# Gate and up projections of a SwiGLU network on one core: eight of eleven chunks computed with the weights stationary, their results kept in columns

## The chip, the cores and the metric

The kernel runs on one core of one Trainium2 chip. The metric is the time of one execution in device microseconds; of three runs of the kernel before the median is 706.38 us (705.44 to 707.03). A profile is one execution, recorded instruction by instruction.

## The reference

Two transformer layers over 256 rows of 1024 channels, all in float32. Each layer is an attention block, a layer norm, a SwiGLU network and a second layer norm. The change touches only the network:

```
def swiglu(h, wg, wu, wd):                      # h 256x1024, wg and wu 1024x2816, wd 2816x1024
    return (jax.nn.silu(h @ wg) * (h @ wu)) @ wd
```

## The kernel before

**Precision.** Float32 accuracy is had from three products of a rounded type: every operand is split into hi (rounded to fp32r) and lo (the rest), and `product` (L969 to L973) issues hi x hi, hi x lo and lo x hi into the same place of PSUM. Each `nc.tensor.matmul(dst, stationary, moving)` loads a 128x128 stationary block into the array (LDWEIGHTS, the profile's engine PEld) and streams the columns of the moving operand through it (MATMUL, engine PE). The profile's names put the moving operand first: `ps<-w_hi,a_lo` is a product that moves w_hi past stationary a_lo.

**The stream of weights.** All weights come from one array of units of 128x2048 values (1 MB). SyncE loads unit u into `raw[u % 3]`; ScalarE rounds it to `w_hi` (`round_unit`, L389); VectorE forms `w_lo` (`rest_of_unit`, L650); TensorE uses it and raises `w_used`. Three slots are in use in turn. Each engine has its own program; their order is only set by the semaphores in it.

**The network.** `ffn` stands once per engine (ScalarE L556, VectorE L910, TensorE L1210) and runs twice, once per layer. The hidden width 2816 is cut into 11 chunks (NFC) of 256. A chunk c takes three units: two of gate and up weights (one for each half of the 1024 channels; in each unit four k tiles of 128 channels, each with 256 gate and 256 up columns), and one of down weights. The activations, already turned, lie as `a_hi`/`a_lo[channel, half, k tile, row]`, half being one of two groups of 128 rows.

For one chunk TensorE issues, before the change:

- `chunk` (L994): for each unit, each half and each k tile, a product with the activations stationary and 512 columns of weights moving: 2 x 2 x 4 x 3 = 48 matmuls of 512 columns. Results have rows on partitions: PSUM bank 0 is half 0, bank 1 is half 1, each with 256 gate and 256 up values.
- `down` (L1218) of the chunk before, with the hidden values stationary: 2 x 2 x 2 x 3 = 24 matmuls of 512 columns into banks 4 to 7, which sum over all chunks.
- `turn_hidden` (L1226): four transposes (128x128, `nc.tensor.transpose` at L1230) that bring the hidden rows of this chunk into columns, as the down product needs them, in PSUM bank 2 (`hT_ps`).

ScalarE takes the silu of the gate half (`silu_of`, L558), VectorE multiplies it by the up half into `h_rows` (`hidden`, L911), TensorE turns, ScalarE rounds the turned values from PSUM into `h_hi` (`hidden_hi`, L562), VectorE forms `h_lo` (`hidden_lo`, L916). Between these each of them rounds the next units, in a fixed order: unit j=2, silu or hidden, unit j=3, hi or lo, unit j=4. Chunks 2 to 9 are one hardware loop on TensorE (`step`, L1233, under `pe.Fori`, L1256), chunks 1 to 9 one on ScalarE (L577) and VectorE (L931). Chunks 0, 1 and 10 are written out.

Of the kernel before, what the change touches and what calls it, by code (L numbers as in the profile page):

```python
# [21 lines left out]
S = 256  # L22
# [4 lines left out]
HALF = 2  # L27
# [31 lines left out]
def build(nc, x_rows, x_cols, stream, w_gates, w1, w2, cpos, positions, norms, out):  # L59
# [8 lines left out]
    with ExitStack() as ctx:  # L68
# [184 lines left out]

        set_ps = ps[:, 4:6, :].rearrange("p b (t r) -> p (b t) r", r=S)
        hT_ps = ps[:, 2, :].rearrange("p (h t r) -> p h t r", h=HALF, t=2)

        def out_ps(t):

# [124 lines left out]
        def _(act):  # L383
            units = [0]

            def copy(dst, src, scale=1.0):
                return nc.scalar.activation(dst, src, ACT.Copy, scale=scale)  # L387
# [168 lines left out]
            def ffn(u0, c0):  # L556

                def silu_of(c, whole):  # L558
                    act.wait_ge(w_used, whole)
                    nc.scalar.activation(silu[:, :, :], ps[:, 0:2, 0:FC], ACT.Silu).then_inc(silu_ready, 1)  # L560

                def hidden_hi(c, hi=h_hi):  # L562
                    act.wait_ge(hT_done, c0 + c + 1)
                    copy(hi[:, :, :, :], hT_ps).then_inc(h_hi_ready, 1)

                def round_in(c, j):

                    round_unit((u0 + j) % SLOTS, ((u0 + j) // SLOTS + 1) * 16 + c * 16, 3 * c + (u0 + j - 2))

                act.wait_ge(first_sums, u0 // U_FF1 + 1)  # L570
                nc.scalar.activation(silu[:, 0, :], ps[:, 0, 0:FC], ACT.Silu).then_inc(first_silu, 1)
                act.wait_ge(w_used, u0 + 2)
                nc.scalar.activation(silu[:, 1, :], ps[:, 1, 0:FC], ACT.Silu).then_inc(silu_ready, 1)
                round_to(u0 + 4)
                hidden_hi(0)
                round_to(u0 + 5)
                with act.Fori(1, NFC - 1) as c:  # L577
                    round_in(c, 2)
                    silu_of(c, 3 * c + (u0 + 1))
                    round_in(c, 3)  # L580
                    hidden_hi(c)
                    round_in(c, 4)
                units[0] = u0 + 3 * (NFC - 1) + 2
                c = NFC - 1
                round_to(u0 + 3 * c + 3)
                silu_of(c, u0 + 3 * c + 1)
                hidden_hi(c, last_hi)
                round_to(min(UNITS, u0 + 3 * c + 5))

            def nsa_values():  # L590
# [41 lines left out]
        def _(dve):  # L632
# [21 lines left out]
            def rest_to(end):  # L654
                for u in range(units[0], end):
                    rest_of_unit(u % SLOTS, u + 1)
                units[0] = max(units[0], end)
# [252 lines left out]
            def ffn(u0, c0):  # L910
                def hidden(c):  # L911
                    dve.wait_ge(silu_ready, c0 + c + 1)
                    nc.vector.tensor_tensor(h_rows[:, :, :], silu[:, :, :], ps[:, 0:2, FC:2 * FC],  # L913
                                            ALU.mult).then_inc(h_ready, 1)

                def hidden_lo(c, hi=h_hi, lo=h_lo):  # L916
                    dve.wait_ge(h_hi_ready, c0 + c + 1)
                    minus(lo[:, :, :, :], hT_ps, hi[:, :, :, :].bitcast(f32)).then_inc(h_lo_ready, 1)

                def rest_in(c, j):  # L920

                    rest_of_unit((u0 + j) % SLOTS, 3 * c + (u0 + j + 1))

                dve.wait_ge(first_silu, u0 // U_FF1 + 1)
                nc.vector.tensor_tensor(h_rows[:, 0, :], silu[:, 0, :], ps[:, 0, FC:2 * FC], ALU.mult).then_inc(first_h, 1)
                dve.wait_ge(silu_ready, c0 + 1)
                nc.vector.tensor_tensor(h_rows[:, 1, :], silu[:, 1, :], ps[:, 1, FC:2 * FC], ALU.mult).then_inc(h_ready, 1)
                rest_to(u0 + 4)
                hidden_lo(0)
                rest_to(u0 + 5)  # L930
                with dve.Fori(1, NFC - 1) as c:  # L931
                    rest_in(c, 2)
                    hidden(c)
                    rest_in(c, 3)
                    hidden_lo(c)
                    rest_in(c, 4)
                units[0] = u0 + 3 * (NFC - 1) + 2
                c = NFC - 1
                rest_to(u0 + 3 * c + 3)
                hidden(c)  # L940
                hidden_lo(c, last_hi, last_lo)
                rest_to(min(UNITS, u0 + 3 * c + 4))

# [24 lines left out]
        def _(pe):  # L968
# [25 lines left out]
            def chunk(u, banks, count=None):  # L994


                for unit in range(2):
                    one_unit(u, unit, banks, count=count)
# [211 lines left out]
            def ffn(u0, c0, ready, l):  # L1210
                def down_part(s, half, k, hi, lo, start, stop, c):


                    at = slice(1024 * k + 512 * c, 1024 * k + 512 * (c + 1))
                    return product(ps[:, 4 + 2 * half + c, :], hi[:, half, k, :], lo[:, half, k, :],
                                   w_hi[:, s, at], w_lo[:, s, at], start=start, stop=stop)

                def down(s, start):  # L1218

                    for half in range(HALF):  # L1220
                        for k in range(2):
                            for c in range(2):
                                last = down_part(s, half, k, h_hi, h_lo, start and k == 0, False, c)
                    last.then_inc(w_used, 1)

                def turn_hidden(c):  # L1226
                    pe.wait_ge(h_ready, c0 + c + 1)
                    for half in range(HALF):
                        for t in range(2):
                            last = nc.tensor.transpose(hT_ps[:, half, t, :], h_rows[:, half, P * t:P * (t + 1)], ident[:, :])  # L1230
                    last.then_inc(hT_done, 1)

                def step(c):  # L1233

                    chunk(u0 + 2, (0, 1), count=3 * c + (u0 - 1))
                    pe.wait_ge(h_lo_ready, c0 + c)
                    pe.wait_ge(lo_ready, 3 * c + (u0 + 2))
                    down((u0 + 1) % SLOTS, False)
                    turn_hidden(c)

                first_chunk(u0, ready, l)

                pe.wait_ge(lo_ready, u0 + 3)
                pe.wait_ge(first_h, u0 // U_FF1 + 1)
                rows_by_weights(u0 + 2, 0, 0, 0)
                turn_hidden(0)
                rows_by_weights(u0 + 2, 0, 1, 1).then_inc(w_used, 1)
                pe.wait_ge(lo_ready, u0 + 4)
                for half in range(HALF):
                    last = rows_by_weights(u0 + 3, 1, half, half)  # L1250
                last.then_inc(w_used, 1)
                pe.wait_ge(h_lo_ready, c0 + 1)
                pe.wait_ge(lo_ready, u0 + 5)
                down((u0 + 4) % SLOTS, True)
                turn_hidden(1)
                with pe.Fori(2, NFC - 1) as c:  # L1256
                    step(c)


                c = NFC - 1  # L1260
                s_before, s_last = (u0 + 3 * c + 1) % SLOTS, (u0 + 3 * c + 2) % SLOTS
                chunk(u0 + 3 * c - 1, (0, 1))
                pe.wait_ge(h_lo_ready, c0 + c)
                pe.wait_ge(lo_ready, u0 + 3 * c + 2)
                for cols in range(2):
                    down_part(s_before, 0, 0, h_hi, h_lo, False, False, cols)
                turn_hidden(c)
                for cols in range(2):
                    down_part(s_before, 0, 1, h_hi, h_lo, False, False, cols)
                pe.wait_ge(h_lo_ready, c0 + NFC)  # L1270
                pe.wait_ge(lo_ready, u0 + 3 * NFC)
                for cols in range(2):
                    for k in range(2):
                        last = down_part(s_last, 0, k, last_hi, last_lo, False, k == 1, cols)
                    last.then_inc(sums_done, 1)
                for k in range(2):
                    for cols in range(2):
                        last = down_part(s_before, 1, k, h_hi, h_lo, False, False, cols)
                last.then_inc(w_used, 1)
                for cols in range(2):  # L1280
                    for k in range(2):
                        last = down_part(s_last, 1, k, last_hi, last_lo, False, k == 1, cols)
                    last.then_inc(sums_done if cols == 0 else w_used, 1)
                if l + 1 < 3:
                    turn_x(l + 1, 0)
# [121 lines left out]
```

## Time and profile before

| | before |
|---|---|
| median of three runs | 706.38 us (705.44 to 707.03) |
| span of the profiled execution | 704.3 us; its own time is not given apart from the span |
| TensorE (PE) busy | 675.0 us, 96% |
| weight loads (PEld) busy | 545.7 us, 77% |
| VectorE (DVE) busy | 405.2 us, 58% |
| ScalarE (ACT) busy | 307.6 us, 44% |
| mean DMA rate | 160 GB/s |

The span runs from the first to the last instruction. Busy is the union of the recorded instructions of an engine. A record of a matmul begins when the instruction is taken up and its end is modelled, so consecutive matmuls overlap in the records: what one costs is the distance between the starts of two neighbours, here called the pitch, and not its length. PE and PEld work side by side.

### The profile page before, as it was taken

The page shows a single profiled execution, that of the slowest core. Times are in us where ns is not written, and L with a number is a line of the kernel's source. Part 1 is how long each engine was busy: PE and PEld are TensorE (multiplying, and loading weights), DVE is VectorE, ACT ScalarE, POOL GpSimd, SP SyncE. Part 2 cuts the span into 40 slices and gives each one's busy share as a digit, 9 for nine tenths or more (in the row PEclk, how much of TensorE's full clock was granted, in tenths as well). Part 3 has the DMA queues.
Part 4 walks back from the last instruction along what each step waited for, and adds up shares of the span by engine and source line. Part 5 has one row for each costly group of instructions (what it writes and reads, how often), then busy time and mean ns, then how long its engine had stood idle before and what let it go on. Part 6 is the DMA issues. An engine that isn't in the chain of part 4 may idle for free.

```text
span 704.3 us, 8489 instructions
## 1 busy us (share of the span) xinstructions
PE 675.0 (96%) x3180; PEld 545.7 (77%) x3180; DVE 405.2 (58%) x529; ACT 307.6 (44%) x435; POOL 30.5 (4%) x66
## 2 busy tenths in 40 slices
PE   5899999999999999999998999999989999999995
PEld 4686886778778888888876788778768888888884
DVE  4554377774864444455448656585855455444446
ACT  4633537663353444433343454674344433334430
POOL 4001000000120000000002000000110000000001
PEclk9999989999999999999999999999999999999998
DMA  8954122003355555555443645313246555555501
GB/s 298 422 198 179 61 83 97 1 2 120 119 191 228 185 185 199 198 186 179 179 179 121 239 180 180 137 43 106 97 165 244 200 197 186 179 182 185 201 27 60
DMA packets 18282, 112.97 MB, mean 160 GB/s; under 512 B 2768, under 2 KB 3024, under 8 KB 5584
## 3 DMA queue, kind: packets, MB, share of 16 engines
q1 hardware_dynamic: 16384, 103.18, 40.2%
q10 hardware_dynamic: 720, 5.24, 1.9%
q0 software_dynamic: 1152, 4.19, 1.7%
q8 instruction: 17, 0.28, 0.2%
q14 instruction: 9, 0.07, 0.0%
HBM read 111.56 MB, written 1.05 MB: 160 GB/s over the span
## 4 chain that ended last, share of the span: by engine, by line
PE 84%; DVE 9%; POOL 2%; DMA 2%; ACT 1%; SPq 1%; issue 1%; POOLq 0%; DVEq 0%
PE ps L971 22%; PE ps L972 22%; PE ps L973 22%; PE ps L1128 4%; PE ps L1163 3%; DVE w_lo L648 2%; PE ps L1076 2%; DMA raw<-stream 2%; PE ps L1230 1%; PE ps L1143 1%; DVE bn L864 1%; PE ps L1165 1%; DVE x L859 1%; DVE x L882 1%; POOL rstd L365 1%
## 5 line engine op out<-in xcount | busy, mean ns | idle before, releaser
L648 DVE TENSOR_TENSOR w_lo<-raw,w_hi 128x2048 fp32r<-128x2048 f32 (+1 forms) x98 | 220.1, 2248 | 134.2 <-ACT w_hi L387 133.9
L971 PE MATMUL ps<-w_hi,a_hi 128*128 128x512 f32 x592 | 238.6, 403 | 15.2 <-DVE w_lo L648 11.2
L972 PE MATMUL ps<-w_lo,a_hi 128*128 128x512 f32 x592 | 233.4, 394 | 0.0
L387 ACT ACTIVATE w_hi<-raw 128x2048 fp32r<-128x2048 f32 (+1 forms) x98 | 184.1, 1878 | 112.5 <-PE ps L973 104.7
L973 PE MATMUL ps<-w_hi,a_lo 128*128 128x512 f32 x592 | 233.2, 394 | 0.0
L971 PEld LDWEIGHTS ps<-w_hi,a_hi 128*128 128x128 f32 x592 | 112.8, 191 | 41.9 <-DVE w_lo L648 11.7
L973 PEld LDWEIGHTS ps<-w_hi,a_lo 128*128 128x128 f32 x592 | 112.8, 191 | 24.5
L972 PEld LDWEIGHTS ps<-w_lo,a_hi 128*128 128x128 f32 x592 | 113.1, 191 | 22.1
L971 PE MATMUL ps<-w_hi,h_hi 128*128 128x512 f32 x160 | 62.4, 390 | 0.0
L973 PE MATMUL ps<-w_hi,h_lo 128*128 128x512 f32 x160 | 62.3, 390 | 0.0
L972 PE MATMUL ps<-w_lo,h_hi 128*128 128x512 f32 x160 | 62.2, 389 | 0.0
L560 ACT ACTIVATE arena<-ps 128x512 f32<-128x512 f32 x20 | 12.0, 598 | 70.3 <-PE ps L973 70.3
L513 ACT ACTIVATE arena<-ps,neg_max 128x128 f32<-128x128 f32 (+1 forms) x96 | 39.0, 427 | 3.4 <-DVE neg_max L798 3.3
L387 ACT ACTIVATE h_hi<-ps 128x512 fp32r<-128x512 f32 x20 | 12.0, 599 | 64.5 <-PE ps L1230 64.5
L1128 PE MATMUL ps<-kz,qT 128*128 128x256 f32 (+1 forms) x96 | 37.6, 488 | 0.0
L973 PEld LDWEIGHTS ps<-w_hi,h_lo 128*128 128x128 f32 x160 | 30.0, 188 | 6.2
L972 PEld LDWEIGHTS ps<-w_lo,h_hi 128*128 128x128 f32 x160 | 30.0, 188 | 6.2
L971 PEld LDWEIGHTS ps<-w_hi,h_hi 128*128 128x128 f32 x160 | 30.0, 188 | 6.2
L913 DVE TENSOR_TENSOR arena<-arena,ps 128x512 f32<-128x512 f32 x20 | 13.8, 688 | 36.4 <-ACT arena L560 36.4
L387 ACT ACTIVATE arena<-ps 128x512 f32<-128x512 f32 (+1 forms) x30 | 18.2, 612 | 37.6 <-PE ps L1147 30.2
L648 DVE TENSOR_TENSOR h_lo<-ps,h_hi 128x512 fp32r<-128x512 f32 x20 | 13.8, 691 | 32.1 <-ACT h_hi L387 32.1
L363 POOL TENSOR_SCALAR var_eps<-mean_var 128x1 f32<-128x1 f32 x8 | 6.0, 748 | 603.6 <-DVE mean_var L869 603.6
(146 smaller groups left out, 570.2 us busy)
## 6 DMA issues: line engine op xcount, KB each, us to landing
raw<-stream SPq DMA_DIRECT2D x94, 1024.0 KB, 4.8
gain<-norms POOLq DMA_DIRECT2D x8, 512.0 KB, 5.0
arena<-w ACTq DMA_DIRECT2D x4, 1024.0 KB, 8.4
raw<-stream SPq DMA_DIRECT2D x4, 512.0 KB, 8.0
twice<-x_cols SPq DMA_DIRECT2D x4, 256.0 KB, 7.1
x<-x_rows ACTq DMA_DIRECT2D x1, 1024.0 KB, 4.8
out<-x SPq DMA_DIRECT2D x4, 256.0 KB, 2.0
wg_raw<-w_gates SPq DMA_DIRECT2D x1, 192.0 KB, 9.6
```

The source lines that it names most:

```text
L365: nc.gpsimd.tensor_tensor(rstd[:, l, half:half + 1], var_eps[:, l, half:half + 1], minus_half[:, :], ALU.pow).then_inc(rstd_ready, 1)
L387: return nc.scalar.activation(dst, src, ACT.Copy, scale=scale)
L513: last = nc.scalar.activation(probs[:, b, at:at + keys], ps[:, 2 - 2 * half + b, h * keys:(h + 1) * keys], ACT.Exp, bias=neg_max[:, j0 + i ...
L560: nc.scalar.activation(silu[:, :, :], ps[:, 0:2, 0:FC], ACT.Silu).then_inc(silu_ready, 1)
L648: return nc.vector.tensor_tensor(dst, a, b, ALU.subtract)
L913: nc.vector.tensor_tensor(h_rows[:, :, :], silu[:, :, :], ps[:, 0:2, FC:2 * FC], ALU.mult).then_inc(h_ready, 1)
L971: nc.tensor.matmul(dst, hi, m_hi, start=start, stop=False)
L972: nc.tensor.matmul(dst, hi, m_lo, start=False, stop=False)
L973: return nc.tensor.matmul(dst, lo, m_hi, start=False, stop=stop)
L1076: last = nc.tensor.matmul(ps[0:KV * NCMP, 6, HID * kv:HID * (kv + 1)], blocks[:, kv, j, :, :].rearrange("p g n -> p (g n)"), w1_sb[:, kv, ...
L1128: nc.tensor.matmul(dst, qT[:, q, P * half:P * (half + 1)], kz[:, k, :, 0:keys], start=True, stop=False)
L1163: nc.tensor.matmul(dst, values[:, 0, c], probsT[:, b, S * h:S * (h + 1)], start=j0 > 0 and h == 0, stop=False)
```

## The change

Chunks 2 to 9 of both layers (16 chunks) compute gate and up the other way round. `columns_by_weights` takes a 128x128 block of the weights as the stationary operand and moves the 256 activation columns (both halves, 2 x 128) past it: per k tile four blocks (two of gate, two of up) and three products each, 2 x 4 x 4 x 3 = 96 matmuls of 256 columns for a chunk. Results have the hidden unit on the partition and the row in the column: bank 0 holds gate, bank 1 up. So silu and the product with up give `h_columns`, a view of the same memory as `h_rows`, which is already in the layout that `down` needs, and these chunks have no `turn_hidden`. `h_hi` and `h_lo` are made from it in SBUF, not from PSUM. `columns_hi` on ScalarE waits for the down product of the chunk before (`w_used`), `hidden_columns` on VectorE waits for `columns_lo` of the chunk before (`h_lo_ready`), and TensorE waits for `h_ready` of the chunk before at the start of a step. Chunks 0, 1 and 10 stay as they were; chunk 1 is now written out on ScalarE and VectorE too. `hT_done` now counts three turns for each network.

```diff
--- before.py
+++ after.py
@@ -253,6 +253,9 @@
 
         set_ps = ps[:, 4:6, :].rearrange("p b (t r) -> p (b t) r", r=S)
         hT_ps = ps[:, 2, :].rearrange("p (h t r) -> p h t r", h=HALF, t=2)
+        h_columns = h_rows.rearrange("p t (h r) -> p t h r", h=HALF)
+
+        TURNS = 3
 
         def out_ps(t):
 
@@ -559,9 +562,19 @@
                     act.wait_ge(w_used, whole)
                     nc.scalar.activation(silu[:, :, :], ps[:, 0:2, 0:FC], ACT.Silu).then_inc(silu_ready, 1)
 
-                def hidden_hi(c, hi=h_hi):
-                    act.wait_ge(hT_done, c0 + c + 1)
+                def silu_columns(c):
+                    act.wait_ge(w_used, 3 * c + (u0 + 1))
+                    nc.scalar.activation(silu[:, :, :], ps[:, 0, :].rearrange("p (t r) -> p t r", t=2),
+                                         ACT.Silu).then_inc(silu_ready, 1)
+
+                def hidden_hi(turned_hidden, hi=h_hi):
+                    act.wait_ge(hT_done, turned_hidden)
                     copy(hi[:, :, :, :], hT_ps).then_inc(h_hi_ready, 1)
+
+                def columns_hi(c):
+                    act.wait_ge(h_ready, c0 + c + 1)
+                    act.wait_ge(w_used, 3 * c + (u0 + 2))
+                    copy(h_hi[:, :, :, :].rearrange("p h t r -> p t h r"), h_columns).then_inc(h_hi_ready, 1)
 
                 def round_in(c, j):
 
@@ -572,19 +585,24 @@
                 act.wait_ge(w_used, u0 + 2)
                 nc.scalar.activation(silu[:, 1, :], ps[:, 1, 0:FC], ACT.Silu).then_inc(silu_ready, 1)
                 round_to(u0 + 4)
-                hidden_hi(0)
+                hidden_hi(TURNS * (u0 // U_FF1) + 1)
                 round_to(u0 + 5)
-                with act.Fori(1, NFC - 1) as c:
+                round_in(1, 2)
+                silu_of(1, u0 + 4)
+                round_in(1, 3)
+                hidden_hi(TURNS * (u0 // U_FF1) + 2)
+                round_in(1, 4)
+                with act.Fori(2, NFC - 1) as c:
                     round_in(c, 2)
-                    silu_of(c, 3 * c + (u0 + 1))
+                    silu_columns(c)
                     round_in(c, 3)
-                    hidden_hi(c)
+                    columns_hi(c)
                     round_in(c, 4)
                 units[0] = u0 + 3 * (NFC - 1) + 2
                 c = NFC - 1
                 round_to(u0 + 3 * c + 3)
                 silu_of(c, u0 + 3 * c + 1)
-                hidden_hi(c, last_hi)
+                hidden_hi(TURNS * (u0 // U_FF1) + 3, last_hi)
                 round_to(min(UNITS, u0 + 3 * c + 5))
 
             def nsa_values():
@@ -913,6 +931,18 @@
                     nc.vector.tensor_tensor(h_rows[:, :, :], silu[:, :, :], ps[:, 0:2, FC:2 * FC],
                                             ALU.mult).then_inc(h_ready, 1)
 
+                def hidden_columns(c):
+                    dve.wait_ge(silu_ready, c0 + c + 1)
+                    dve.wait_ge(h_lo_ready, c0 + c)
+                    nc.vector.tensor_tensor(h_columns, silu[:, :, :].rearrange("p t (h r) -> p t h r", h=HALF),
+                                            ps[:, 1, :].rearrange("p (t h r) -> p t h r", t=2, h=HALF),
+                                            ALU.mult).then_inc(h_ready, 1)
+
+                def columns_lo(c):
+                    dve.wait_ge(h_hi_ready, c0 + c + 1)
+                    minus(h_lo[:, :, :, :].rearrange("p h t r -> p t h r"), h_columns,
+                          h_hi[:, :, :, :].rearrange("p h t r -> p t h r").bitcast(f32)).then_inc(h_lo_ready, 1)
+
                 def hidden_lo(c, hi=h_hi, lo=h_lo):
                     dve.wait_ge(h_hi_ready, c0 + c + 1)
                     minus(lo[:, :, :, :], hT_ps, hi[:, :, :, :].bitcast(f32)).then_inc(h_lo_ready, 1)
@@ -928,15 +958,21 @@
                 rest_to(u0 + 4)
                 hidden_lo(0)
                 rest_to(u0 + 5)
-                with dve.Fori(1, NFC - 1) as c:
+                rest_in(1, 2)
+                hidden(1)
+                rest_in(1, 3)
+                hidden_lo(1)
+                rest_in(1, 4)
+                with dve.Fori(2, NFC - 1) as c:
                     rest_in(c, 2)
-                    hidden(c)
+                    hidden_columns(c)
                     rest_in(c, 3)
-                    hidden_lo(c)
+                    columns_lo(c)
                     rest_in(c, 4)
                 units[0] = u0 + 3 * (NFC - 1) + 2
                 c = NFC - 1
                 rest_to(u0 + 3 * c + 3)
+                dve.wait_ge(h_lo_ready, c0 + c)
                 hidden(c)
                 hidden_lo(c, last_hi, last_lo)
                 rest_to(min(UNITS, u0 + 3 * c + 4))
@@ -1230,13 +1266,27 @@
                             last = nc.tensor.transpose(hT_ps[:, half, t, :], h_rows[:, half, P * t:P * (t + 1)], ident[:, :])
                     last.then_inc(hT_done, 1)
 
+                def columns_by_weights(u, unit):
+
+                    s = u % SLOTS
+                    for k in range(4):
+                        kt = 4 * unit + k
+                        for j in range(4):
+                            at = slice(512 * k + P * j, 512 * k + P * (j + 1))
+                            last = product(ps[:, j // 2, S * (j % 2):S * (j % 2 + 1)], w_hi[:, s, at], w_lo[:, s, at],
+                                           a_hi[:, :, kt, :], a_lo[:, :, kt, :], start=kt == 0 and j % 2 == 0,
+                                           stop=kt == KT - 1 and j % 2 == 1)
+                    last.then_inc(w_used, 1)
+
                 def step(c):
 
-                    chunk(u0 + 2, (0, 1), count=3 * c + (u0 - 1))
+                    pe.wait_ge(h_ready, c0 + c)
+                    for unit in range(2):
+                        pe.wait_ge(lo_ready, 3 * c + (u0 + unit))
+                        columns_by_weights(u0 + 2 + unit, unit)
                     pe.wait_ge(h_lo_ready, c0 + c)
                     pe.wait_ge(lo_ready, 3 * c + (u0 + 2))
                     down((u0 + 1) % SLOTS, False)
-                    turn_hidden(c)
 
                 first_chunk(u0, ready, l)
 
@@ -1259,6 +1309,7 @@
 
                 c = NFC - 1
                 s_before, s_last = (u0 + 3 * c + 1) % SLOTS, (u0 + 3 * c + 2) % SLOTS
+                pe.wait_ge(h_ready, c0 + c)
                 chunk(u0 + 3 * c - 1, (0, 1))
                 pe.wait_ge(h_lo_ready, c0 + c)
                 pe.wait_ge(lo_ready, u0 + 3 * c + 2)
```

## Rows read from the trace of the kernel before

**Rows 1.** The page: span, busy time of TensorE, and the chain that ended last.

```profile
span 704.3 us, 8489 instructions
...
PE 675.0 (96%) x3180; PEld 545.7 (77%) x3180; DVE 405.2 (58%) x529; ACT 307.6 (44%) x435; POOL 30.5 (4%) x66
...
PE 84%; DVE 9%; POOL 2%; DMA 2%; ACT 1%; SPq 1%; issue 1%; POOLq 0%; DVEq 0%
```

**Rows 2.** Windows, chunks 2 to 9 of each layer; columns as in the first line.

```profile
core 0: us, PE busy (x) PEld busy (x) DVE busy (x) ACT busy (x) POOL busy (x), PEclk, DMA share, GB/s
217.90:352.40 134.50, 134.50 (x611) 111.33 (x610) 66.07 (x40) 53.80 (x40) 0.00 (x0) 1.00 0.53 187
538.30:672.80 134.50, 134.50 (x612) 111.33 (x610) 66.07 (x40) 53.80 (x40) 0.00 (x0) 1.00 0.52 187
```

**Rows 3.** Timeline of PE, one chunk of the loop: start us, length us.

```profile
251.38 0.60 PE L1230 MATMUL ps<-ident,arena 128*128 128x128 f32 x4
251.73 0.48 PE L971 MATMUL ps<-w_hi,a_hi 128*128 128x512 f32 x1
252.05 0.40 PE L972 MATMUL ps<-w_lo,a_hi 128*128 128x512 f32 x1
...
252.52 0.40 PE L971 MATMUL ps<-w_hi,a_hi 128*128 128x512 f32 x1
...
254.36 0.39 PE L973 MATMUL ps<-w_hi,a_lo 128*128 128x512 f32 x1
...
267.96 0.39 PE L973 MATMUL ps<-w_hi,h_lo 128*128 128x512 f32 x1
268.19 0.60 PE L1230 MATMUL ps<-ident,arena 128*128 128x128 f32 x4
```

**Rows 4.** Timeline of ScalarE and VectorE in two chunks of the loop.

```profile
246.13 0.60 ACT L560 ACTIVATE arena<-ps 128x512 f32<-128x512 f32 x1 [3.52 <-PE ps L973]
246.76 0.69 DVE L913 TENSOR_TENSOR arena<-arena,ps 128x512 f32<-128x512 f32 x1 [1.83 <-ACT arena L560]
252.01 0.60 ACT L387 ACTIVATE h_hi<-ps 128x512 fp32r<-128x512 f32 x1 [3.48 <-PE ps L1230]
252.65 0.69 DVE L648 TENSOR_TENSOR h_lo<-ps,h_hi 128x512 fp32r<-128x512 f32 x1 [1.78 <-ACT h_hi L387]
254.45 2.29 DVE L648 TENSOR_TENSOR w_lo<-raw,w_hi 128x2048 fp32r<-128x2048 f32 x1 [1.11 <-ACT w_hi L387]
```

**Rows 5.** Timeline, products with 48 moving columns (the gates of the attention).

```profile
32.81 0.19 PEld L973 LDWEIGHTS ps<-wg_hi,a_lo 128*128 128x128 f32 x1
32.84 0.27 PE L973 MATMUL ps<-wg_hi,a_lo 128*128 128x48 f32 x1
32.92 0.19 PEld L971 LDWEIGHTS ps<-wg_hi,a_hi 128*128 128x128 f32 x1
...
33.71 0.19 PEld L972 LDWEIGHTS ps<-wg_lo,a_hi 128*128 128x128 f32 x1
```

**Rows 6.** Timeline of PE in the attention: plain f32 and bf16 products.

```profile
113.01 0.38 PE L1165 MATMUL ps<-arena 128*128 128x128 f32 x2
113.23 0.60 PE L1128 MATMUL ps<-kz,qT 128*128 128x256 f32 x2
113.66 0.27 PE L1130 MATMUL ps<-causal,ident_b 128*128 128x256 bf16 x1
113.77 0.59 PE L1128 MATMUL ps<-kz,qT 128*128 128x512 f32 x1
```

**Rows 7.** The loads of those products: the groups of PEld by shape, x is their number.

```profile
L1165 PEld LDWEIGHTS ps<-arena 128*128 128x128 f32 x96 | 18.2, 190 | 2.5
```

**Rows 8.** A window in which the granted clock is 0.50; columns as in rows 2.

```profile
387.96:391.37 3.41, 3.41 (x9) 2.64 (x10) 2.69 (x2) 0.00 (x0) 0.00 (x0) 0.50 0.72 285
```

**Rows 9.** Timeline of PE in that window.

```profile
388.37 0.63 PE L972 MATMUL ps<-w_lo,a_hi 128*128 128x512 f32 x1
...
390.93 0.60 PE L972 MATMUL ps<-w_lo,a_hi 128*128 128x512 f32 x1
```

## The prediction

> **What bounds the kernel now.** I read the page first: span 704.3 us, TensorE busy for 675.0 us of it and 84% of the chain that ended last [rows 1]. The reader is to see that no other engine is near: VectorE has 58%, ScalarE 44%. But a mean over stages doesn't price a change to one of them, so next the windows: in the loop over chunks 2 to 9, both layers, PE is busy for 134.50 of 134.50 us, VectorE for 66.07, ScalarE for 53.80, the DMA share is 0.53 and the granted clock 1.00, the upper level, 2.4 GHz [rows 2]. TensorE never waits there. So the change is worth what it does to TensorE's own instruction stream in 2 x 134.5 us, and nothing else, as long as no wait opens.
>
> Busy time says nothing of what a matmul costs, so the third view is the timeline: start to start. From the first turn of one chunk (251.38) to that of the next (268.19) are 16.81 us [rows 3]. In between stand 4 turns and 72 matmuls of 512 columns. From the 12th of these (254.36) to the 72nd (267.96) are 60 steps in 13.60 us: a pitch of 226.7 ns [rows 3]. 512 columns at 2.4 GHz are 213.3 ns, so each matmul pays 13.4 ns beyond its columns. On these 13.4 ns the forecast hangs.
>
> **What goes.** 72 x 226.7 ns = 16.32 us; the chunk takes 16.81; so the four turns and the switch around them cost 0.49 us [rows 3]: 0.35 from the first turn to the next matmul (251.38 to 251.73), 0.09 because that matmul takes 0.32 instead of 0.23, and 0.05 in the ten or so that follow. 16 chunks: 7.8 us. All of it lies on the path, since PE never rests [rows 2]. The turns wait for nothing now, so no stall goes with them. If the slow matmuls after a switch remain (the shape still switches twice in a chunk, 512 to 256 and back), 0.05 us stay per switch: 0.8 to 1.6 us less gain. I take zero and keep 1.6 for the range.
>
> **What comes.** 48 matmuls of 512 columns become 96 of 256, three products for each of 32 (block, k tile) pairs. The columns are the same, 24,576 per chunk; the number of matmuls and of weight loads doubles. In 16 chunks 768 matmuls at 226.7 ns = 174.1 us become 1536 at a pitch p. With the turns gone,
>
> change of the time = 1536 x p - 174.1 - 7.8 us.
>
> No row shows an fp32r matmul of 256 columns, so p is bounded from the nearest rows.
>
> - *The load.* Each matmul needs a load of 128 columns of 32 bits. With only 48 columns moving, eight loads take 32.81 to 33.71: 112 ns each [rows 5]. That is the load's own pace, and p can't be under it. It does hide behind a matmul: in the attention two f32 matmuls of 128 columns with such loads (190 ns long in the record) take 113.01 to 113.23, 110 ns each [rows 6, 7], where a pass over 128 f32 columns costs half of the 256-column pass, itself 0.43 / 2 = 215 ns [rows 6]. Load and stream, both about 107 ns, run side by side at full overlap. It is just this balance that the changed chunks will have.
> - *The stream.* 256 columns at 2.4 GHz are 106.7 ns. A bf16 matmul of 256 columns takes 113.66 to 113.77, 110 ns, with the load of a f32 matmul behind it [rows 6]. So 256 columns in full-rate mode aren't slow as such.
> - *The 13.4 ns.* They are seen with fp32r at the full clock only. At a granted clock of 0.50 (1.2 GHz) the same matmul of 512 columns takes 388.37 to 390.93 for six, 426.7 ns [rows 8, 9], which is 512 / 1.2 with nothing over. The f32 pass of 256 columns at full clock, two cycles for a column, takes 215 ns against 213 [rows 6]. So the extra is no work of the array: it shows only when the array draws 32-bit columns at 2.4 GHz, and hides as soon as it draws half as fast. Either what feeds the columns needs a restart for each instruction that a slower array doesn't notice (a fixed 13.4 ns for each matmul, p = 120.1), or it feeds 6% too slowly (in proportion, p = 113.3).
>
> I take the fixed cost. A feed that is too slow by just 6% for a clock that differs twofold from the next one would be a coincidence; an instruction's start that has slack at half rate and none at full rate is what the three rows ask for. Both ends stay: 112 ns (load bound) and, above, 128 (below).
>
> Sum: 1536 x 120.1 ns = 184.5 us; 184.5 - 174.1 - 7.8 = +2.6 us. The changed chunk takes 96 x 0.120 + 24 x 0.2267 = 16.97 us against 16.81. The doubled number of starts costs 0.64 us in a chunk, more than the 0.49 that the turns gave.
>
> The Trainium skill (TensorE: Matmul & The Clock Gate, Back-to-back issue gap) gives N / 2.4 + 2.5 ns for a warm matmul, a fixed part too, but a small one. The bf16 row agrees with it within the timeline's 10 ns [rows 6]; the fp32r stream doesn't: 226.7 against 215.8 ns [rows 3]. By that rule p would be 109 ns, under the load's 112, so the load would decide: this is the second rival.
>
> **Edits that I price at nothing.** Silu, the product, hi and lo keep their number and size (128x512: 0.60, 0.69, 0.60, 0.69 us [rows 4]); two of them now read SBUF instead of PSUM, whose price the trace doesn't show for ScalarE. They have room. The new wait of `columns_hi` for the down product ends at about the time of the old one: `h_hi` starts at 252.01 behind four turns that start at 251.38, as the down product ends [rows 3, 4]. `h_lo` is there by 253.34, and the down product that needs it starts 48 matmuls after 251.73, at 262.7: 9 us of cover [rows 3, 4]. Behind the waiting `columns_hi` on ScalarE stands the rounding of unit j=4, and VectorE's rest of it, done at 256.74 [rows 4] and needed at 262.7 also: 6 us of cover. TensorE's new wait for `h_ready`: `hidden` ends at 247.45 [rows 4], the step begins at 251.7, 4 us of cover; behind it would stand the whole step. `hidden_columns` waits for `columns_lo` of the chunk before, an instruction ahead of it in VectorE's own order. Units are used in the same order at the same times within 2%, so SyncE's loads, 0.53 of the DMA time [rows 2], don't move. If one such cover failed, each us would be paid 16 times; I see none within 4 us of failing.
>
> **Rivals.**
>
> 1. *In proportion (faster).* p = 113.3: the streams stay at 174.1 and the 7.8 us of turns are pure gain: -7.8, 698.6 us. For it: 226.7 is 17/16 of 213.3, and a rate is the simplest reading of one size. Against: the two half-rate rows above.
> 2. *Load bound (faster).* The extra belongs to matmuls longer than their load, or is small; p = 112: 172.0 - 174.1 - 7.8 = -9.9, 696.5 us. For it: the f32 and bf16 rows at 110 [rows 6]. Against: nothing there draws fp32r.
> 3. *Never settled (slower).* The matmuls behind a switch run late: the 12th starts at 254.36, where ten pitches from the second, at 252.05, would give 254.32, and the two steps from 252.05 to 252.52 take 235 ns each, 21.7 over the columns [rows 3]. The stream takes some ten matmuls to reach its even pace, at which each load begins with the matmul before it and has 120 ns of slack. With 256 columns moving there is no slack: load 112, stream 107. If the pace after a switch is the pace throughout, p = 106.7 + 21.7 = 128: 196.6 - 174.1 - 7.8 = +14.7, 721 us. It decides for slower from p = 118.4 on, where the turns are used up. TensorE's instruction supply would work in the same direction: pairs of load and matmul stand at 110 ns only in short runs here [rows 5, 6], and the change asks for 96 at 120.
> 4. *Loads in the open.* p = 107 + 112 = 219: 336.4 - 174.1 - 7.8 = +154, 861 us. The rows speak against it: 226.7 is far less than 213 + 112 [rows 3, 5], and two of 110 ns hold a load and a pass each [rows 6]. The Trainium skill (TensorE: Matmul & The Clock Gate, The mechanism) says that a weight load overlaps a running matmul only where it goes to other rows of the array, and here all rows are used both times; by that rule this rival would be the forecast. The trace contradicts it.
>
> That the change doesn't do what it says could only mean that turns stay; the steps have none left, so I give that no chance.
>
> **How the numbers follow.** The sum is a difference, made in the profiled execution (704.3 us of span); the median of the runs is 706.38, 2.1 us higher, and the difference is put on it. Fixed cost, with p from 118.5 to 124: 0.40, forecast 706.38 + 2.6 = 709.0. In proportion: 0.23. Load bound: 0.12. Never settled, p over 124: 0.19. Loads in the open: 0.02. Something that cancels (p from 117.5 to 118.5, or a mix): 0.04. What a measurement can tell from no change is about 0.2%, 1.4 us, so same means p between 117.5 and 119.3; part of the fixed case lies there. Faster: 0.23 + 0.12 + 0.02 = 0.37. Same: 0.08. Slower: 0.55. The range: down to the load bound's 696.5, up to the never-settled 721, leaving half of each tail out. The forecast's own range, p from 118.5 to 124, is 706.5 to 715.
>
> **What would show it.** In the changed timeline the start-to-start of 256-column matmuls in the middle of a step: 120 ns right, 113 or 112 the first or second rival, 128 the third. The period of a chunk, between matmuls of the same place: 16.97 us against 16.81. PE busy throughout the loop's windows: the covers held. No L1230 between chunk 1 and chunk 10. If PE shows idle time before the first matmul of a step, a wait that I priced at nothing is the cause and the forecast is wrong in that step; if the pitch of the 512-column matmuls of `down` moves from 226.7, my fixed price is no property of a matmul, and the reasoning falls even if the sum should hold.

## The result, and the profile after

The changed kernel takes 707.91 us (median of 18 runs, 705.28 to 709.92) against 705.46 us of the kernel before (18 runs beside it): 2.5 us more by the medians. The ratio on record, which need not be the quotient of the two medians, is 1.0044, with a 95% interval of 1.0026 to 1.0061: 3.1 us slower, 1.8 to 4.3. The forecast was 2.6 us slower.

The page of the changed kernel, against [rows 1]:

```profile
span 705.2 us, 9901 instructions
...
PE 675.5 (96%) x3884; PEld 577.7 (82%) x3884; DVE 405.2 (57%) x529; ACT 307.9 (44%) x435; POOL 30.4 (4%) x66
...
PE 84%; DVE 9%; POOL 2%; DMA 2%; ACT 1%; SPq 1%; issue 1%; POOLq 0%; DVEq 0%
```

There are 704 more matmuls and as many more loads (768 more, and 64 turns fewer); VectorE and ScalarE are as they were. The page can't show more: its span is only 0.9 us longer. The windows by stage do. Chunks 2 to 9 of both layers, the stage between the two, the start, and one chunk (columns as in [rows 2]):

```profile
219.36:355.28 135.92, 135.92 (x963) 128.25 (x962) 66.09 (x40) 53.98 (x40) 0.00 (x0) 1.00 0.51 185
537.92:673.83 135.91, 135.91 (x963) 128.25 (x962) 66.08 (x40) 54.01 (x40) 0.00 (x0) 1.00 0.51 185
355.28:523.85 168.57, 162.13 (x773) 129.17 (x772) 111.25 (x163) 80.64 (x129) 9.04 (x12) 1.00 0.41 150
0.00:75.73 75.73, 64.16 (x308) 50.22 (x308) 35.03 (x47) 32.02 (x32) 10.80 (x43) 0.98 0.66 255
236.42:253.40 16.98, 16.98 (x121) 16.02 (x120) 8.26 (x5) 6.75 (x5) 0.00 (x0) 1.00 0.50 185
```

The same stages of the kernel before, as far as the groups ahead don't hold them:

```profile
352.55:524.41 171.86, 165.44 (x775) 131.58 (x774) 111.27 (x163) 80.68 (x129) 9.05 (x12) 0.98 0.41 147
0.00:74.46 74.46, 63.23 (x308) 49.53 (x309) 35.06 (x47) 32.07 (x32) 10.82 (x43) 1.00 0.69 259
218.13:352.55 134.42, 134.42 (x611) 111.25 (x610) 66.07 (x40) 53.80 (x40) 0.00 (x0) 1.00 0.53 187
538.50:672.93 134.43, 134.43 (x611) 111.26 (x610) 66.07 (x40) 53.80 (x40) 0.00 (x0) 1.00 0.52 187
```

The reader is to see that PE is busy for all of 135.92 us, so no wait opened, and that the changed stage grew from 134.42 to 135.92 us, in the second layer from 134.43 to 135.91 (+2.98 in all), which lies inside the measured 1.8 to 4.3. The stages that didn't change differ too. The one between the layers has -3.29 us, and PE's busy time alone has -3.31 (162.13 against 165.44); the start has +1.27, of which PE's busy time has 0.93. The same matmuls took another time because the granted clock was another (1.00 against 0.98 between the layers, 0.98 against 1.00 at the start): the spells at 1.2 GHz fall in other places from one execution to the next. Comparing the spans of two executions would have hidden two thirds of the effect.

The timeline of PE in one changed chunk, against [rows 3]:

```profile
236.42 0.28 PE L1007 MATMUL ps<-a_hi,w_hi 128*128 128x256 f32 x1
236.53 0.28 PE L1008 MATMUL ps<-a_lo,w_hi 128*128 128x256 f32 x1
...
247.81 0.28 PE L1009 MATMUL ps<-a_hi,w_lo 128*128 128x256 f32 x1
247.93 0.40 PE L1007 MATMUL ps<-w_hi,h_hi 128*128 128x512 f32 x1
...
250.45 0.39 PE L1009 MATMUL ps<-w_hi,h_lo 128*128 128x512 f32 x1
...
253.17 0.39 PE L1009 MATMUL ps<-w_hi,h_lo 128*128 128x512 f32 x1
253.40 0.28 PE L1007 MATMUL ps<-a_hi,w_hi 128*128 128x256 f32 x1
```

From the 2nd to the 96th, 94 steps in 11.28 us: 120.0 ns. The down product keeps its 24 matmuls, in 5.47 us, and from 250.45 to 253.17 they have the pitch of before: 12 steps in 2.72 us, 226.7 ns. No turn stands at 253.40. The period, from the first matmul of a chunk to the first of the next, is 16.98 us, 0.17 more than before.

ScalarE and VectorE in the same chunk, against [rows 4]:

```profile
248.13 0.60 ACT L567 ACTIVATE arena<-ps 128x512 f32<-128x512 f32 x1 [3.85 <-PE ps L1009]
248.76 0.69 DVE L937 TENSOR_TENSOR arena<-arena,ps 128x512 f32<-128x512 f32 x1 [2.15 <-ACT arena L567]
253.60 0.63 ACT L390 ACTIVATE h_hi<-arena 128x512 fp32r<-128x512 f32 x1 [3.07 <-PE ps L1009]
254.26 0.69 DVE L666 TENSOR_TENSOR h_lo<-arena,h_hi 128x512 fp32r<-128x512 f32 x1 [1.40 <-ACT h_hi L390]
256.07 2.29 DVE L666 TENSOR_TENSOR w_lo<-raw,w_hi 128x2048 fp32r<-128x2048 f32 x1 [1.11 <-ACT w_hi L390]
```

`h_hi` from SBUF takes 0.63 us instead of 0.60. The product with up (L937) ends at 249.45, 4 us ahead of the step at 253.40; `h_lo` ends at 254.95, 10 us ahead of the down product that uses it (264.91), and the rest of unit j=4 at 258.36, 6.5 us ahead of the same. The covers held.

### The profile page after: what moved, and what is told of

Read it like the earlier page. It is cut to its first block, busy times and chain, and to the rows that moved or that the text cites. A ratio compares the mean times of both kernels' runs of the same rounds, so it can differ in the third digit from the quotient of the medians.

```text
span 705.2 us, 9901 instructions
## 1 busy us (share of the span) xinstructions
PE 675.5 (96%) x3884; PEld 577.7 (82%) x3884; DVE 405.2 (57%) x529; ACT 307.9 (44%) x435; POOL 30.4 (4%) x66
## 4 chain that ended last, share of the span: by engine, by line
PE 84%; DVE 9%; POOL 2%; DMA 2%; ACT 1%; SPq 1%; issue 1%; POOLq 0%; DVEq 0%
PE ps L1007 23%; PE ps L1009 22%; PE ps L1008 22%; PE ps L1164 4%; PE ps L1199 3%; DVE w_lo L666 2%; PE ps L1112 2%; DMA raw<-stream 2%; PE ps L1179 1%; DVE bn L882 1%; PE ps L1201 1%; DVE x L877 1%; DVE x L900 1%; POOL rstd L368 1%; DVE a_lo L666 1%
## 5 line engine op out<-in xcount | busy, mean ns | idle before, releaser
L1007 PE MATMUL ps<-w_hi,a_hi 128*128 128x512 f32 x336 | 136.3, 406 | 15.6 <-DVE w_lo L666 11.6
L1007 PE MATMUL ps<-a_hi,w_hi 128*128 128x256 f32 x512 | 145.0, 283 | 0.0
L1009 PE MATMUL ps<-a_hi,w_lo 128*128 128x256 f32 x512 | 144.9, 283 | 0.0
L1008 PE MATMUL ps<-a_lo,w_hi 128*128 128x256 f32 x512 | 144.9, 283 | 0.0
L1009 PE MATMUL ps<-w_hi,a_lo 128*128 128x512 f32 x336 | 133.0, 396 | 0.0
L1008 PE MATMUL ps<-w_lo,a_hi 128*128 128x512 f32 x336 | 132.8, 395 | 0.0
L1008 PEld LDWEIGHTS ps<-a_lo,w_hi 128*128 128x128 f32 x512 | 98.2, 192 | 0.5
L1007 PEld LDWEIGHTS ps<-a_hi,w_hi 128*128 128x128 f32 x512 | 98.2, 192 | 0.5
L1009 PEld LDWEIGHTS ps<-a_hi,w_lo 128*128 128x128 f32 x512 | 98.2, 192 | 0.0
L1009 PEld LDWEIGHTS ps<-w_hi,a_lo 128*128 128x128 f32 x336 | 64.1, 191 | 14.0
```

What stands on the lines that cost most here:

```text
L1007: nc.tensor.matmul(dst, hi, m_hi, start=start, stop=False)
L1008: nc.tensor.matmul(dst, hi, m_lo, start=False, stop=False)
L1009: return nc.tensor.matmul(dst, lo, m_hi, start=False, stop=stop)
```

## The experiments

Each was made from one of the two kernels; times are compared with the kernel before on the same chip. Where one execution was taken, the verdict rests on the pitch, or on the period of a chunk, and not on the time. From the second chunk of a layer on the period repeats within 0.01 us, with half loads in the kernel before within 0.04. Where a run computes only a part of the chunks or takes other operands, only its time is read. In the cuts from the edits, `...` stands for what is left out.

**The turns back in the changed kernel.**

```diff
                     down((u0 + 1) % SLOTS, False)
+                    pe.wait_ge(h_ready, c0 + c + 1)
+                    for half in range(HALF):
+                        for t in range(2):
+                            nc.tensor.transpose(hT_ps[:, half, t, :], h_rows[:, half, P * t:P * (t + 1)], ident[:, :])
```

> The changed kernel with four turns put back at the end of each step of chunks 2 to 9 (their result goes to bank 2 and isn't used). Theory of the forecast, that turns and the switch around them cost 0.49 us and the doubled starts 0.64 us of a chunk: period 16.98 + 0.45 to 0.49 = 17.43 to 17.47 us, time 7.2 to 7.8 us above the changed kernel, 1.5% above the kernel before. Rival, that the turns were nearly free because the switch between shapes costs the same with and without them (the changed kernel still switches twice): period up by 0.35 or less, 5.6 us or less.

Measured 714.74 us, ratio 1.0144 (1.0118 to 1.0171). The windows of two chunks:

```profile
219.24:236.66 17.42, 17.42 (x128) 16.41 (x126) 8.25 (x5) 6.87 (x6) 0.00 (x0) 1.00 0.52 182
236.66:254.07 17.41, 17.41 (x128) 16.40 (x126) 8.26 (x5) 6.75 (x6) 0.00 (x0) 1.00 0.51 181
```

The second, 17.41, is 0.43 over 16.98: just under what was expected (0.45 to 0.49) and over the rival's 0.35. The timeline splits it into 0.35 from the first turn to the next matmul and 0.08 because that matmul takes 0.20 instead of 0.12. (The first chunk of a layer stands behind the turns of chunk 1 in the changed kernel too, where it takes 17.06, 219.36 to 236.42; so 17.42 isn't to be compared with 16.98.) By the two ratios the time is 1.0% or 7 us above the changed kernel. The turns were no free work.

**The turns out of the kernel before.**

```diff
+                def stale_hi(c):
+                    act.wait_ge(w_used, 3 * c + (u0 + 2))
+                    copy(h_hi[:, :, :, :], hT_ps).then_inc(h_hi_ready, 1)
...
-                    hidden_hi(c)
+                    stale_hi(c)
...
                 def step(c):
 
+                    pe.wait_ge(h_ready, c0 + c)
...
-                    turn_hidden(c)
```

> The kernel before with the turns of chunks 2 to 9 left out and nothing else: the down products of these chunks use hidden values of chunk 1 that still stand in bank 2, so that part of the computation is left out. Theory of the forecast: the period falls from 16.81 to 72 x 226.7 ns = 16.32 us, 7.8 us faster than the kernel before, a ratio of 0.989. Rival (the turns hide behind the matmuls, or uncover a wait for the weights): a period of 16.6 to 16.81, 0 to 3 us faster.

Measured 695.56 us, ratio 0.9877 (0.9851 to 0.9904). A window of one chunk:

```profile
249.98:266.30 16.32, 16.32 (x74) 13.51 (x72) 8.26 (x5) 6.72 (x5) 0.00 (x0) 1.00 0.56 193
```

16.32 us, as worked out from the pitch. The ratio gives 8.7 us (6.8 to 10.5), which holds the 7.8 expected. So the turns are worth 0.49 us a chunk, and the 96 short matmuls in place of 48 long ones cost the 0.66 us between 16.32 and 16.98: 0.64 by the two pitches (96 x 120.0 - 48 x 226.7 ns), and 0.02 at the change of shape.

**One run of 256 moving columns in place of two of 128.**

```diff
-                                           a_hi[:, :, kt, :], a_lo[:, :, kt, :], ...
+                                           a_hi[:, 0, min(kt, 6):min(kt, 6) + 2, :], a_lo[:, 0, min(kt, 6):min(kt, 6) + 2, :], ...
```

> The changed kernel with the 256 moving columns taken from two neighbouring k tiles of one half, one run of 256 in place of two runs of 128 (so gate and up of chunks 2 to 9 are products with other activations). Theory (a fixed price for each matmul): a pitch of 120.0 ns as in the changed kernel. Rival (the price is for each run of addresses, or the two runs add to it): the pitch falls, to 113 if half of the 13.3 ns belongs to each run; time 10 us less.

Measured in one execution: 708.09 us; the timeline of PE, 2nd and 96th matmul of a chunk:

```profile
253.20 0.28 PE L1008 MATMUL ps<-a_lo,w_hi 128*128 128x256 f32 x1
...
264.48 0.28 PE L1009 MATMUL ps<-a_hi,w_lo 128*128 128x256 f32 x1
```

11.28 / 94 = 120.0 ns. Whether the 256 columns are one run of addresses or two makes no difference.

**384 moving columns.** The same edit with three k tiles, `ps[:, j // 2, 0:384]` as the target.

> The changed kernel with 384 moving columns in one run in place of 256 (other activations, results over one another). Theory (columns at 2.4 GHz plus 13.3 ns): 173.3 ns, the kernel 82 us longer than the changed one, 789 us. Rival (the stream is 17/16 too slow, which 512 fits as well, and 256 is set by the load): 170.0 ns, 5 us less than that.

Measured 787.87 us in one execution. The 8th and the 96th matmul:

```profile
263.25 0.33 PE L1008 MATMUL ps<-a_lo,w_hi 128*128 128x384 f32 x1
...
278.50 0.33 PE L1009 MATMUL ps<-a_hi,w_lo 128*128 128x384 f32 x1
```

15.25 / 88 = 173.3 ns, that is 384 / 2.4 = 160.0, and 13.3. With 256 (120.0) and 512 (226.7) three sizes lie on one line: the columns at 2.4 GHz, and 13.3 ns for each matmul. The rival's proportion (170.0) is out.

**128 moving columns, twice as many matmuls.** Each product of the changed chunks is issued once for each half.

> The changed kernel with each matmul of 256 columns cut into two of 128 (192 matmuls of 128 columns for a chunk). Theory: the stream would take 53.3 + 13.3 = 66.7 ns, so the load decides, 111 to 112 ns; a chunk takes 192 x 0.112 + 5.44 = 26.9 us, the kernel about 160 us more than the changed one, 867 us. Rival (price of the start adds to the load, the two don't overlap): 112 + 13 = 125 ns, 40 us more than that.

Measured 866.13 us in one execution; a chunk takes 26.94 us:

```profile
271.64:298.58 26.94, 26.94 (x218) 25.95 (x216) 8.26 (x5) 6.75 (x5) 0.00 (x0) 1.00 0.33 117
```

From the 2nd to the 192nd matmul of this chunk (271.70 to 292.91) are 190 steps in 21.21 us, 111.6 ns. 128 columns and the 13.3 ns would be 66.7, so something else sets the pitch: the load's own pace, the 112 of [rows 5]. Nothing is added to it; the rival's 125 is out.

**Half of the load.** Stationary blocks of 64 columns, everything else alike.

```diff
-                            at = slice(512 * k + P * j, 512 * k + P * (j + 1))
-                            last = product(ps[:, j // 2, ...
+                            at = slice(512 * k + P * j, 512 * k + P * j + 64)
+                            last = product(ps[0:64, j // 2, ...
```

> The changed kernel with stationary blocks of 64 columns in place of 128 in the changed chunks (half of gate and up isn't computed), the moving columns and the number of matmuls the same. Theory (the 13.3 ns belong to the moving stream's start): the pitch stays at 120.0 ns although the load is half as long. Rival (with 256 columns the load fills the pitch and sets it, 112 ns and something for the handover, and the agreement with 106.7 + 13.3 is chance): the pitch falls, to 113.3 by the proportion or 109 without any price, 10 to 17 us less.

Measured 695.13 us in one execution. The 2nd and the 96th matmul of a chunk:

```profile
250.35 0.28 PE L1008 MATMUL ps<-a_lo,w_hi 128*64 128x256 f32 x1
...
261.01 0.28 PE L1009 MATMUL ps<-a_hi,w_lo 128*64 128x256 f32 x1
```

10.66 / 94 = 113.4 ns. This speaks against the forecast's reading: the moving stream is the same, and half of the 13.3 ns is gone. The edit halves two things at once, though: what is loaded, and the partitions of PSUM that a matmul writes (64 in place of 128). No run parts them while fp32r moves. The value that the rival named came true, though its reading (a load that sets the pitch) doesn't fit 384 and 512 columns.

**The changed chunks in bf16.** Weights and activations as `.bitcast(bf16)`, every other element.

> The changed kernel with weights and activations of the changed chunks read as bf16 (the upper half of each value, every other element, so the low parts of the products lose their worth). Theory (the price belongs to 32-bit columns at the full clock): 109 to 110 ns, 15 to 17 us less than the changed kernel, about 692 us. Rival (any matmul of 256 full-rate columns beside a load of 128 pays it in a long stream, and the single bf16 matmul in the attention didn't show it): 120 ns, no change.

Measured 701.52 us in one execution, with a mean granted clock of 0.984 against 0.989 in the changed kernel, so the time says little. The 2nd and the 96th matmul of a chunk:

```profile
253.34 0.27 PE L1008 MATMUL ps<-a_lo,w_hi 128*128 128x256 bf16 x1
...
263.99 0.28 PE L1009 MATMUL ps<-a_hi,w_lo 128*128 128x256 bf16 x1
```

10.65 / 94 = 113.3 ns. Neither theory: a long bf16 stream pays 6.7 ns, which the single bf16 matmul of [rows 6], read as one step of 0.11 us, couldn't show. Single steps at a change of type also mislead: the step out of this bf16 stream is 0.03 us (263.99 to 264.02) and the one behind it 0.32. So the price isn't that of 32-bit columns alone. Both operands are read here with a stride of two elements; whether that has a part wasn't tested. With the half loads it made a new theory: the load's bytes set it.

**A quarter of the load.** As above, with 32 columns.

> The changed kernel with stationary blocks of 32 columns in the changed chunks (three quarters of gate and up aren't computed). Theory now (the extra over the columns is the load's: 13.3 ns for 128 columns of 32 bits, 6.7 for 64 columns, 6.7 for 128 columns of 16 bits, so one cycle of 2.4 GHz for each 16 bytes that a partition's load reads): 106.7 + 3.3 = 110.0 ns, a period of about 10.56 + 5.44 + 0.03 = 16.03 us, the kernel 15 us under the changed one. Rival (two levels, a slow and a fast one, and 64 columns already had the fast one): 113.3 ns as with 64 columns, 10 us under.

Measured 707.65 us in one execution, clock 0.984. The 3rd and the 96th matmul of a chunk:

```profile
254.06 0.28 PE L1009 MATMUL ps<-a_hi,w_lo 128*32 128x256 f32 x1
...
265.02 0.28 PE L1009 MATMUL ps<-a_hi,w_lo 128*32 128x256 f32 x1
```

10.96 / 93 = 117.8 ns, 11.2 over the columns: more than with 64 columns. Both theories fall (110.0 and 113.3).

**Half of the load in the kernel before.** Stationary blocks of 64 rows, 512 columns moving: `product(ps[0:64, half, :], a_hi[:, half, kt, 0:64], a_lo[:, half, kt, 0:64], ...)`.

> The kernel before with stationary blocks of 64 rows in gate and up of chunks 2 to 9 (half of the rows aren't computed), 512 weight columns moving as before. Theory (the extra is the load's): 213.3 + 6.7 = 220.0 ns in place of 226.7, a period of 16.49 us, 5 us under the kernel before. Rival (the forecast's reading: 13.4 ns for the start of each 32-bit stream, whatever is loaded): 226.7 ns, a period of 16.81 us, no change.

Measured 707.75 us in one execution. The 3rd and the 48th matmul of a chunk:

```profile
252.15 0.39 PE L973 MATMUL ps<-w_hi,a_lo 128*64 128x512 f32 x1
...
262.49 0.39 PE L973 MATMUL ps<-w_hi,a_lo 128*64 128x512 f32 x1
```

10.34 / 45 = 229.8 ns, more than the 226.7 with the whole load, and the period rose from 16.81 to 16.92 and 16.96 us. Both fall again (220.0 and 226.7). A narrower stationary block, with a shorter load and fewer partitions written, can make the stream slower.

**The wide kernel.** `a_hi` and `a_lo` in one tile, so that a block of w_hi needs one matmul. The order of the blocks changes too: all k tiles of a block come before the next block.

```diff
+                            nc.tensor.matmul(ps[:, j, :], w_hi[:, s, at], a_both[:, :, :, kt, :], start=kt == 0, stop=False)
+                            last = nc.tensor.matmul(ps[:, j, 0:S], w_lo[:, s, at], a_hi[:, :, kt, :], start=False, stop=kt == KT - 1)
```

> The changed kernel with a_hi and a_lo side by side in one tile, so that a stationary block of w_hi takes one matmul of 512 moving columns (a_hi and a_lo) into a bank of its own, and a block of w_lo one of 256 into the first half of that bank; ScalarE copies the second halves out, VectorE adds them. 64 matmuls for a chunk in place of 96, the same columns. Theory (13.3 ns for each fp32r matmul, whatever its size): 32 x (226.7 + 120.0) = 11.09 us instead of 11.52, a period of 16.54 to 16.57 us, 6.6 to 7 us under the changed kernel and 3.9 us under the kernel before, ratio 0.9945. Rival, that the price goes by columns or by time and not by starts (then 120 and 227 are two shapes' own prices and moving runs of 128 cost extra): period 16.8 or more, no gain on the kernel before. A second rival is a new wait: the two copies and two additions make the hidden values about 2 us later; TensorE needs them 5.4 us after the last gate or up product, so no idle time is expected, and if there is some it stands before the first matmul of a step.

Measured 703.55 us (12 runs), ratio 0.9986 (0.9958 to 1.0014): no change clear of noise against the kernel before. The theory missed; the period is 16.79 us, the rival's. The timeline shows where:

```profile
256.90 0.40 PE L1293 MATMUL ps<-a_both,w_hi 128*128 128x512 f32 x1
257.14 0.28 PE L1294 MATMUL ps<-a_both,w_lo 128*128 128x256 f32 x1
257.26 0.40 PE L1293 MATMUL ps<-a_both,w_hi 128*128 128x512 f32 x1
...
257.96 0.40 PE L1293 MATMUL ps<-a_both,w_hi 128*128 128x512 f32 x1
```

Three pairs take 1.06 us, 353.3 ns each and not 346.7. PE is busy for all of the 16.79 us: the added copies and sums are covered.

**The wide kernel with like shapes in a row.** Same matmuls; the 16 of 512 columns of a unit together, the 16 of 256 together.

```diff
+                    for part in ((0, 1) if unit == 0 else (1, 0)):
+                        for j in (0, 1, 3, 2):
...
+                            for k in range(4):
```

> The wide kernel (one matmul of 512 moving columns for a block of w_hi, one of 256 for a block of w_lo) with the order changed: in the first unit of a chunk all 16 matmuls of 512 columns and then all 16 of 256, in the second all 16 of 256 and then all 16 of 512. Theory (a run of like shapes goes at the even pace of 226.7 and 120.0 ns, and the 353 ns of a mixed pair are the price of alternating): 32 x 346.7 = 11.09 us and some 0.05 us for each of two switches, a period of 16.55 to 16.65 us, 3 to 4 us under the kernel before, ratio 0.995. Rival (the four runs of 128 columns of the moving operand, or the writes to a whole bank, cost the 6.7 ns): 233 ns in the runs of 512, a period of 16.75 to 16.8 us, the time of the kernel before.

Measured 702.92 us (12 runs), ratio 0.9951 (0.9923 to 0.9979): 3.5 us faster than the kernel before (1.5 to 5.4; 2.4 by the medians), and so faster than the changed kernel too. The window of one chunk and, in the timeline, its runs:

```profile
237.81:254.36 16.55, 16.55 (x89) 14.35 (x88) 9.54 (x8) 7.88 (x7) 0.00 (x0) 1.00 0.53 190
```

```profile
237.81 3.79 PE L1295 MATMUL ps<-a_both,w_hi 128*128 128x512 f32 x16
241.44 4.00 PE L1298 MATMUL ps<-a_both,w_lo 128*128 128x256 f32 x32
245.27 3.82 PE L1295 MATMUL ps<-a_both,w_hi 128*128 128x512 f32 x16
```

3.63 us for 16 is 226.9 ns, 3.83 for 32 is 119.7. The second run of 512 columns, behind one of 256, takes 3.65 us (to 248.92), 228 ns. The matmuls are those of the wide kernel and only their order is another, so the 6.7 ns of a mixed pair were the price of alternating; moving operands made of four runs of 128 columns, and results that fill a whole bank, cost nothing.

## Why the prediction was right, and where it wasn't

- *TensorE's stream alone decides.* Right: PE busy for 135.92 of 135.92 us in the changed stage, and its growth (2.98 us) lies inside the measured 1.8 to 4.3.
- *What goes.* Forecast 0.49 us a chunk, 7.8 us. Taking the turns out of the kernel before gave 16.32 instead of 16.81, the same 0.49; putting them into the changed kernel cost 0.43.
- *The switch that remains.* Taken as zero, with 1.6 us as bound. 96 x 120.0 + 24 x 226.7 ns are 16.96 us; the period is 16.98, the 0.02 being in the down product, which takes 5.47 us and not 24 x 226.7 ns = 5.44. The first chunk of each layer, still behind the turns of chunk 1, takes 0.08 more. Together 0.5 us (16 x 0.02 + 2 x 0.08), most of the distance between the forecast's 2.6 and the stages' 2.98, once the pitch that was forecast 0.1 ns too long has taken 0.15 off.
- *What comes.* p = 120.1 was forecast, 120.0 measured; 384 columns (173.3) confirm the form, a fixed 13.3 ns beside the columns. The rivals at 112, 113.3, 128 and 219 ns are excluded by the same rows; the one that never settles had 256 columns leave the load no slack, and the trace has steps of 0.12 us from the second on. The Trainium skill's N / 2.4 + 2.5 ns (TensorE: Matmul & The Clock Gate, Back-to-back issue gap), which the page gives for a matmul without a load beside it, has the form, and the trace doesn't agree with the constant: 13.3 ns in fp32r, 6.7 in bf16 here. The Trainium skill's rule that a load overlaps a running matmul only in other rows of the array (TensorE: Matmul & The Clock Gate, The mechanism) is contradicted: a load at 112 ns and a stream of 107 ns fit into 120. The same section also lets a load go ahead into a background weight buffer, and with that the trace agrees.
- *Why 13.3.* Here the forecast was wrong in its reason. It called the extra a restart of the feed of 32-bit columns, the same for each matmul whatever is loaded. But bf16 pays 6.7 ns too. And with the moving stream unchanged, the extra goes with the width of the stationary block: 13.3 ns for 128 columns, 6.7 for 64 and 11.2 for 32; with 512 columns moving it is 13.3 for 128 and 16.5 for 64. Whether that is the load's doing or that of the partitions written isn't parted: the bf16 run, with all 128 partitions written and loads of half the recorded length, pays 6.7 too, but its moving stream is another as well. The 48 or 96 matmuls of the two kernels have the same block of 128 x 128; that the constant carried over from 512 to 256 columns is measured, but the forecast's reason for it doesn't hold, and so far its number was luck. The likeliest rival reading, that shorter loads are cheaper in proportion to their bytes, fell as well.
- *Edits at nothing.* Right; the covers are where they were priced.

What stays open is what sets the extra. It isn't monotone in the width of the block, nor in the length that the profile gives the loads (192, 134 and 108 ns for 128, 64 and 32 columns, 97 in bf16). It differs between a run of one shape and an alternation (16.7 ns a matmul in the mixed pairs, (353.3 - 320.0) / 2). The stream of 512 columns reaches its even value only some ten matmuls behind a switch, in both kernels, while that of 256 has it from the second step on. That looks like two streams that fall into step with each other; this is argued, not shown.

## What to carry to other kernels

Price a reshaped matmul stream by start-to-start distances of a run of one shape, as columns over the clock plus a constant per matmul that the same loads have in the trace, and count the matmuls as well as the columns: here doubling their number (0.66 us a chunk) cost more than the four transposes (0.49 us) that it saved. To need fewer matmuls, put operands with the same stationary block side by side in the moving operand, and keep like shapes in a row. Measure such a change by its stage: what the spells of the lower clock moved elsewhere (3.3 us) was larger than the effect.

## What the runs showed of the hardware that was not expected

- At the full clock, back-to-back fp32r matmuls with loads of 128x128 cost columns / 2.4 GHz + 13.3 ns (256, 384, 512 columns: 120.0, 173.3, 226.7 ns), and never less than the load's own 111.6 ns (128 columns).
- A narrower stationary block isn't always less time: 256 columns moving past blocks of 128, 64, 32 columns take 120.0, 113.4, 117.8 ns; 512 columns past blocks of 128 and 64 take 226.7 and 229.8.
- Alternating matmuls of 512 and 256 columns costs 6.7 ns a pair over the same matmuls in runs of 16 and 32. In the two wide kernels that is a period of 16.79 or 16.55 us, 3.8 us in 16 chunks.
